# RWKV output and attention key projections computed token block by token block in a two-layer fp32 decoder kernel

## What is computed

```python
# end of the RWKV time mix: y (1, T, 16, 64), per head group norm, gate, output projection, residual
mean = jnp.mean(y, axis=-1, keepdims=True)
var = jnp.mean(jnp.square(y - mean), axis=-1, keepdims=True)
y = ((y - mean) * lax.rsqrt(var + GN_EPS)).reshape(B, T, D) * gn_w + gn_b
y = (y + bonus.reshape(B, T, D)) * jax.nn.silu(gp)
x = x + y.astype(h.dtype) @ w_out
...
# start of the attention: residual norm, four projections, head norms and rotary turns on k and q
kv = rms_norm(x, norm_kv) @ w_kv            # k and v
proj = rms_norm(x, norm_b) @ w_in           # q and gate
k = partial_rope(rms_norm(k, k_norm), cos, sin)
q = partial_rope(rms_norm(q, q_norm), cos, sin)
```

## Time and profile before

| | |
|---|---|
| median of 3 runs | 1151.72 us (1151.21 to 1154.56) |
| profiled execution, its own time | 1154.9 us |
| its span in the trace | 1153.1 us |
| busy PE / DVE / ACT | 93% / 63% / 43% of the span |
| mean granted TensorE clock | 0.969 of full |
| loads | 95 panels of 2 MB, 202.55 MB on the queue of SP |

### The profile page before, as it was taken

How to read it: one execution, slowest core, us unless ns; L and a number is a source line. 1 busy time by engine, 2 the same in 40 slices (tenths; PEclk the granted TensorE clock), 3 DMA queues, 4 the chain that set the end, 5 groups by cost and what they waited for, 6 DMA issues and landing times.

```text
span 1153.1 us, 19629 instructions
## 1 busy us (share of the span) xinstructions
PE 1071.2 (93%) x8492; PEld 896.8 (78%) x8492; DVE 728.1 (63%) x1145; ACT 499.0 (43%) x774; POOL 33.3 (3%) x31
## 2 busy tenths in 40 slices
PE   5999999897899979999988999999899798999997
PEld 5885679895688767787766989999557678999995
DVE  6778328649579777656485786777435855554544
ACT  2433041225344575444354544545233645554442
POOL 0000033200000100000000000000000000000000
PEclk9999999998999998999988999999899998999999
DMA  9762302502565430555245477767634544474520
GB/s 388 274 255 92 129 2 97 201 5 74 219 222 216 150 143 2 219 219 206 87 146 219 180 274 293 275 228 289 233 126 167 233 147 167 164 281 166 211 74 37
DMA packets 15078, 204.88 MB, mean 178 GB/s; under 512 B 1800, under 2 KB 1800, under 8 KB 2832
## 3 DMA queue, kind: packets, MB, share of 16 engines
q1 hardware_dynamic: 14544, 202.55, 46.2%
q10 hardware_dynamic: 448, 1.08, 0.2%
HBM read 202.57 MB, written 1.05 MB: 177 GB/s over the span
## 4 chain that ended last, share of the span: by engine, by line
PE 80%; DVE 12%; ACT 3%; issue 2%; DMA 2%; SPq 0%; DVEq 0%; ACTq 0%
PE bank L433 15%; PE bank L435 15%; PE bank L434 15%; PE bank L491 7%; PE bank L392 5%; PE bank L707 5%; PE bank L504 2%; DVE slot_parts L1770 2%; PE bank L518 2%; DMA ring<-in_stream 1%; PE bank L612 1%; PE bank L691 1%; DVE arena L2180 1%; DVE small L1744 1%; ACT page_parts L1201 1%
## 5 line engine op out<-in xcount | busy, mean ns | idle before, releaser
L433 PE MATMUL bank<-page_parts 128*128 128x512 f32 (+1 forms) x1104 | 378.3, 343 | 5.1 <-DVE page_parts L1803 2.8
L1770 DVE TENSOR_TENSOR slot_parts<-ring,page_parts 128x2048 fp32r<-128x2048 f32 x104 | 237.2, 2290 | 125.8 <-ACT page_parts L1201 125.4
L1201 ACT ACTIVATE page_parts<-ring 128x2048 fp32r<-128x2048 f32 x104 | 197.8, 1911 | 138.2 <-PE bank L435 90.3
L433 PEld LDWEIGHTS bank<-page_parts 128*128 128x128 f32 x1104 | 210.3, 191 | 29.9 <-issue 4.5
L435 PE MATMUL bank<-page_parts 128*128 128x512 f32 x576 | 225.6, 392 | 0.0
L434 PE MATMUL bank<-slot_parts,page_parts 128*128 128x512 f32 x576 | 225.6, 392 | 0.0
L1258 ACT ACTIVATE arena<-bank 128x512 f32<-128x512 f32 (+2 forms) x138 | 76.4, 574 | 202.6 <-PE bank L491 70.4
L434 PE MATMUL bank<-page_parts 128*128 128x256 f32 x528 | 149.4, 283 | 0.0
L435 PE MATMUL bank<-page_parts,slot_parts 128*128 128x256 f32 x528 | 149.4, 283 | 0.0
L435 PEld LDWEIGHTS bank<-page_parts 128*128 128x128 f32 x576 | 109.0, 189 | 23.2
L434 PEld LDWEIGHTS bank<-slot_parts,page_parts 128*128 128x128 f32 x576 | 109.3, 190 | 21.7
(11 more groups left out here) (284 smaller groups left out, 1225.5 us busy)
## 6 DMA issues: line engine op xcount, KB each, us to landing
ring<-in_stream SPq DMA_DIRECT2D x95, 2048.0 KB, 8.3
arena<-in_x SPq DMA_DIRECT2D x2, 512.0 KB, 4.2
gn<-in_gn ACTq DMA_DIRECT2D x2, 512.0 KB, 12.8
out<-arena SPq DMA_DIRECT2D x2, 512.0 KB, 2.6
cc<-in_consts SPq DMA_DIRECT2D x1, 898.5 KB, 6.4
pc<-in_params SPq DMA_DIRECT2D x1, 287.5 KB, 6.6
gn<-in_head_sel ACTq DMA_DIRECT2D x1, 32.0 KB
pos_i<-in_positions ACTq DMA_DIRECT2D x1, 1.0 KB, 3.9
```

The costliest lines, as they stand in the source:

```text
L433: mm(out, a[0], b[0], start=start, stop=False)
L1201: act(unit_parts(n)[0], unit_values(n)[1], ACT.Copy).then_inc(ac.step("w_hi"), 1)
L1770: tt(unit_parts(n)[1], lo, hi, ALU.subtract).then_inc(dv.step("w_lo"), 1)
```

## The change

wo_a and k1 go through a new function, `split_blocks`: both halves (four units) are multiplied with block 0, then both halves again with block 1. `turn_block` transposes one block of y or x, into two banks of four feature tiles, at a given place between the dozens. So block 1 of y is finished, and block 0 of x added, normed and cut, while PE multiplies.

What goes with it:

- the group norm of a block takes its root on ACT (`group_root`) and refines it on DVE: five small instructions instead of twelve;
- `norm_block`, `add_to_x(name, (tb,))` and `x_block` do the residual norm of one block;
- the high parts of y and x are written by ACT straight from PSUM (`halves_of`, and 16 copies of 128x128 for each block of x), the low parts by DVE straight from PSUM (`lows_of`, and 16 instructions of 128x128);
- the panels of wo_a and of k1 are held until block 1 has used them; both projections have four pages for high parts;
- the second direct ada panel becomes a summed one. Its turn on DVE comes before the head norm of K1, that of the next one between the norms of K1 and Q1, and a second column sum stands behind v1.

```diff
@@ TensorE
+            def split_blocks(name, src, pages, split, between=None):
+
+                first, panels_of = len(units), []
+                for half in range(2):
+                    split_panel((name, half), pages, by_k=True)
+                    panels_of.append(order[-1])
+                for tb in range(TB):
+                    bs = [claim((name, half, tb)) for half in range(2)]
+                    for n in range(4):
+                        half, i = divmod(n, 2)
+                        if between:
+                            between(tb, n)
+                        W = use_unit() if tb == 0 else unit_parts(first + n)
+                        if half == 0:
+                            pe.wait_ge(*evacuated((split, tb, i)))
+                        for k in range(4 * i, 4 * i + 4):
+                            ins = three(bs[half][:, :], [a[:, k, tb * P:(tb + 1) * P] for a in src],
+                                        [w[:, k - 4 * i, :] for w in W], k == 0, k == KT - 1)
...
+                        if tb:
+                            units[first + n]["used"] = pn.last
+                            panels_of[half][1] = pn.last
...
-            transposes("yT", Yr, ready=lambda i: (sem("y_gated"), 3 + i // 2))
-            ada_turned()
+            turn_block("yT", Yr, 0, lambda g: (sem("y_gated"), g + 1))
             stage[0] = "attention"
-            for half in range(2):
-                split_tok(("wo_a", half), split_parts(Y_PAGES), (13, 5, 7, 10), wait=("yT_split", 0) if half == 0 else None)
-
-
-            ada_direct()
-            pe.wait_ge(sem("xn"), 4)
-            transposes("hT_b", XN)
-            ada_turned()
-            stage[0] = "attention"
+
+            def beside_wo_a(tb, n):
+
+                if (tb, n) == (0, 1):
+                    ada_turned()
+                elif (tb, n) == (1, 0):
+                    turn_block("yT", Yr, 1, lambda g: (sem("y_gated"), 2 + g + 1))
+                elif (tb, n) == (1, 2):
+                    turn_block("hT_b", XN, 0, lambda g: (sem("xn"), 3))
+
+            def beside_k1(tb, n):
+
+                if (tb, n) == (0, 2):
+                    turn_block("hT_b", XN, 1, lambda g: (sem("xn"), 4))
...
-                if name in ("k1", "v1"):
-                    ada(1)
-                elif name == "q1":
-                    ada(0, rest=1)
+                if name != "g1":
+                    ada(1, rest=int(name != "k1"))
@@ ScalarE
+            def group_root(tb):
+
+                act_.wait_ge(sem("y_reduced"), 2 * tb + 2)
+                act(gn_root[:, tb, :], stat2[:, tb, :], ACT.Sqrt, scale=1.0 / HD, bias=con("gn_eps")).then_inc(ac.step("gn_root"), 1)
...
+                for g in range(2):
+                    act_.wait_ge(*finished(("hT_b", tb, g)))
+                    for jj in range(4):
+                        j = 4 * g + jj
+                        for pages, w in ((HKV_PAGES, "norm_kv"), (HB_PAGES, "norm_b")):
+                            act(split_parts(pages)[0][:, j, tb * P:(tb + 1) * P], bank(("hT_b", tb, g))[:, jj * P:(jj + 1) * P], ACT.Copy,
+                                scale=par(w)[:, j:j + 1]).then_inc(ac.step("hT_b_hi"), 1)
@@ VectorE
+            reduced(0)
             gated(0)
             group_norm(0)
             split(unit_of["wo_a", 0] + 1)
+            reduced(1)
+            lows_of("yT", 0, Y_PAGES)
+            split(unit_of["wo_a", 0] + 2)
             gated(1)
             group_norm(1)
-            split_output("wo_a", "yT", Y_PAGES)
-            split(unit_of["k1", 0] + 1)
-            add_to_x("wo_a")
-
-
-            norm()
-
-            split_h("hT_b", HKV_PAGES, HB_PAGES)
-            for _ in range(4):
+            lows_of("yT", 1, Y_PAGES)
+            for tb in range(TB):
+                add_to_x("wo_a", (tb,))
+                split(unit_of["k1", 0] + 2 * tb)
+                norm_block(tb)
+                split(unit_of["k1", 0] + 2 * tb + 1)
+                for g in range(2):
+                    dve.wait_ge(sem("hT_b_hi"), 16 * tb + 8 * g + 8)
...
+            for _ in range(2):
                 next_unit(("k1", 0, 0))
             ada(KT)
...
+                if name == "k1":
+                    ada(KT)
```

130 lines of the change are left out of this document (90 added, 40 removed).

## The result

The changed kernel takes 1135.22 us (median of 4 runs, 1134.22 to 1138.4) against 1152.82 us before (4 runs, 1151.21 to 1154.56): ratio 0.9855, 95% interval 0.983 to 0.988. The profiled execution took 1135.88 us with a span of 1134.1 and a mean granted clock of 0.980.

What follows compares the result with a forecast made beforehand. TensorE was taken to bound the kernel (80% of the span). Stops 4.6, half clock 2.1 and direct panel 4.6, less column sum 0.8, gave 10.5 us: 1151.7 to 1141.2 us, range 1137 to 1148.

Steps and rivals of the forecast that it cites:

- The stops: TensorE from wo_a to g1: 12.4 us of standing still falls to 7.8, a gain of 4.6 us.
- the wrong bound: ACT's 128x128 copies of x: at most 0.373 us each, at least 0.19; 0.30 taken, nearer the upper bound.
- v1's stop: TensorE waits 3.3 us in v1 for a weight's low part, because VectorE works back to back behind k1.
- The wait for q1's second panel: Behind k1: load issued at 313.7, landing 8.3 us later, so VectorE waits 1.6 us for its high part.
- The half clock of the earlier trace: Behind the old 8.2 us stop before y's transposes: half clock costs 2.1 us, which the change gains.
- The term of 4.6 less 0.8: Between wo_a and k1: dropping the second direct panel saves TensorE 4.6 us, an added column sum costs 0.8.
- The local sum: Up to the attention's start: stops, half clock and direct panel less column sum gain 10.5 us.
- Behind that nothing changes but bank numbers: From the attention's start on: no further effect, so the 10.5 us gain is kept.
- rival 1: Short stops cost more than counted, with slow pieces and half clock: gain about 4 us, 1147.5; chance 0.20.
- Rival 2: The stop in v1 does not come and x is cut early: gain 14 to 15 us, 1137; chance 0.09.
- Rival 3: A later stage waiting for loads takes the gain back: within 3.5 us of before, 1150; chance 0.08.
- rival 4: wo_a's and k1's panels held too long, q1's second panel loads late: slower, 1155 at a 22.3 us load; chance 0.05.

Runs made afterwards that it cites:

- narrow_sum: Changed kernel, the summed panel between K1's and Q1's norm multiplying only 8 of its 512 columns in seven of eight steps: 1134.09 us, ratio 0.9835.
- after_tail: Changed kernel with the bank rotation set to 172 at the attention's start, so every later product has the bank of the kernel before: 1142.35 us, ratio 0.9900.
- after_again: Changed kernel, unedited, measured and profiled a second time: 1135.73 us, ratio 0.9856.
- before_sum: Kernel before with only its second direct panel replaced by a summed one on VectorE between K1's and Q1's norm: 1161.95 us, ratio 1.0071.
- direct_back: Changed kernel with the second panel of the conditioning product computed on TensorE again, between wo_a and k1: 1150.45 us, ratio 0.9978 to the kernel before.
- after_bank: Changed kernel with banks shifted only for the direct panel before wo_c (bank 1 again) and the transposes behind it: 1141.12 us, ratio 0.9888.
- ada_mid: Changed kernel with VectorE's summed panel moved behind the first two weight units of Q1's norm: 1141.77 us, ratio 0.9921.

## Why the prediction was right here and wrong there

**The stops.** Predicted 1.2, 1.1, 0.5, 1.3, 3.3 and 0.4, sum 7.8; measured 1.25, 1.05, none, 0.29, 3.65, none, sum 6.2. For block 0 of x I had counted 5.4 us for both engines; PE took 5.7 from its first product of block 1 of y to the turn (284.57 to 290.28), DVE 5.1 from its additions to the end of the norm (285.03 to 290.13), so DVE was there in time. For block 1 of x it is the 128x128 pieces that were cheaper: sixteen high parts on ACT in 4.24 us, 0.265 each where I took 0.30, nearer to the wrong bound (on DVE 0.264, I had 0.27).

v1's stop and its nearest reason (VectorE without a gap) were as told, but loads have a part in it. The wait for q1's second panel came as counted: issued at 314.56, its high part begun at 322.89, DVE still for 1.91 us where I had 1.6. For that load the prediction worked out 6.8 us by a fit of the Trainium skill, DMA: Bandwidth & Descriptors, section Anatomy of one DMA; there the fit is for transfers issued by GpSimd, while SP issues these, and 8.3 was right. A second load I hadn't counted: v1's first panel is issued when the first summed panel has released its slot, at 320.44, 0.44 behind another load, and lands after 14.3 us. Its high part is ready just when DVE comes to it (336.7). Had DVE been earlier, it would have stood still there, so that the stop came out at nearly my number is partly luck. narrow_sum, which has the same loads and no stop, shows that the panel between K1 and Q1 is needed for the stop, not that the loads cost nothing.

**The clock.** The half clock of the earlier trace rows went, as counted (2.1). I had not counted a new one, and in the changed kernel's first execution there is one behind v1's stop, 6.8 us long. It isn't fixed to the stop. In after_tail the same stop of 3.67 us left the clock at 1.00, and in after_again, with 3.13 us, it fell for 3.4 us:

```profile
353.50:364.00 10.50, 6.83 (x31) 5.68 (x31) 10.09 (x15) 3.52 (x3) 0.00 (x0) 1.00 1.00 390
```

(That is after_tail; the same window of the changed kernel has 0.67.) The Trainium skill, TensorE: Matmul & The Clock Gate, part 1, lets the gate follow how busy PE has been lately. These rows agree in so far as no stop of 1.25 or 1.05 was followed by half clock and some of 3.1 to 3.7 were; the length of the stop alone doesn't decide it.

**The direct panel.** The term of 4.6 less 0.8 is right only inside the change. before_sum shows that alone the exchange costs 8.2 us, direct_back that undoing it in the changed kernel costs 8.0 in A, where the panel also takes a slot and so delays a load. My sum treated as additive what was one exchange: blocks give PE work to do under the norm, and only then does the panel stop being a useful filler and its slot become the one that k1 needs.

**The local sum.** 10.5 predicted. A is 141.0 to 144.5 (mean 142.9) in the four executions with the code of before, and 130.3 to 132.3 (mean 131.1) in the five with that of the changed kernel: 11.8. after_tail and after_bank say 11.5 and 12.9 by their ratios; they measured 1142.35 and 1141.12 us, where the forecast of 1141.2 stood. So near a hit is partly luck. In the two first executions A differs by 9.4: the stops gave 6.3 and the panel less the column sum 3.8, but half clock outside the stops cost 2.2 us before (half of 4.3 us) and 2.7 after, so it gave nothing back. Stops 1.6 smaller than counted and a half clock that I had not counted nearly cancelled. Over the four and five executions the terms are 6.1 (stops), 2.3 (clock: 3.8 lost before, 1.5 after) and 3.8, together 12.2, near the 11.8. The clock term is the one that varies: 1.6 to 5.7 us before, 0 to 2.7 after.

**The step that failed** is "Behind that nothing changes but bank numbers". It was true of the code and wrong as a reason for zero. One of those numbers puts the direct panel ahead of wo_c on a bank that ACT still reads, and that is worth 3.8 us in the trace and 3.8 to 5.2 by the ratios, although the edit adds a wait there: the granted clock of the stage goes from 0.81 to 0.89 up to 1.00. The Trainium skill, Perfetto Trace Analysis, section Matmuls, asks for rotation through different banks so that a bank's copy overlaps the next product; here the panel that met an uncopied bank is the faster case (28.0 against 31.8), since its wait stands in time that PE would lose anyway. By itself that step takes the forecast from 1141.2 to 1136 or 1137, to the edge of the range; the local gain, 1.3 us above the forecast, does the rest.

**What stays open.** 11.8 and 3.8 make 15.6 of the 17.6 us; the rest lies inside the interval of the ratio (13.8 to 19.6 us). A part of it may be the clock between attention and wo_c, whose length there differs by up to 5 us among executions of the same code. Of rival 1 the stretch of half clock occurred (6.8 us in the first execution), the dear short stops did not. Rival 2 did not: v1's stop came, and the larger gain has another cause. Rival 3 did not, and rival 4 did only in direct_back and ada_mid. Why the clock falls behind v1's stop in one execution and not in another is not shown.

## What to carry to other kernels

"Only the buffer numbers change behind this" is a term of the sum, not a zero: list, for each product behind the edit that has slack, who still holds its new bank. A stop can cost twice where critical work follows it, if that work then runs at the lower clock; ahead of wo_c, work with slack did better behind a stop than ahead of it, as it still ended in time. And a filler that is taken out must be priced in the new order *and* in the old one: here, measured in A, taking the same panel off TensorE lost 11.6 us in the old order and gained 8.0 in the new one.

## What the hardware showed unexpectedly

- The same program differs by 12 us (1146.39 to 1158.63) from one execution to the next, in step with the mean granted clock (0.979 and 0.967; correlation -0.91): one profile of each kernel can be wrong by more than the effect looked for, and an interval cut at rows shows more. B repeats to 0.03 us where the clock stays at 1.00, though only within 2.3 us with bank 1, and A within 2 to 3.5 us.
- Sixteen matmuls of a direct panel take 3.65 us at the full clock, and 5.35 or 6.59 behind a stop of 3.71 us, as the clock comes back earlier or later on the way.
- Stops of 1.25 and 1.05 us left the clock at 1.00. In that of 3.65 it fell to 0.50, in one of 3.67 at the same place in another execution (after_tail) it did not, and behind that of 4.25 sixteen transposes took 3.65 us instead of 2.20.
